# Pages in 32 partitions and dealt v rows in the sample's attention of a hybrid decoder step

## The reference

```
# the expert layer, for a block tb of 128 tokens, 128 chosen experts per token
act = gelu(einsum('thkd,td->thk', expert_u[eid], tb))
y   = einsum('thk,thkd->td', g * act, expert_v[eid])

# the sample's attention: 8 samples, each 32 pages of 128 tokens (256 + 32 words a token) and its new token
ckv_all = concatenate([cache_ckv[page_table].reshape(8, 4096, 256), ckv])
kr_all  = concatenate([cache_krope[page_table].reshape(8, 4096, 32), krope])
s = (q_abs . ckv_all + q_pe . kr_all) * scale        # the mask keeps every one of these tokens
o_lat = softmax(s) . ckv_all
```

## Time and profile before

| | us |
|---|---|
| median of 3 runs | 4161.53 |
| lowest, highest | 4159.66, 4172.78 |
| the profiled execution | 4134.78 |
| its span, first to last instruction | 4133.0 |
| granted clock of PE, mean | 0.918 |

### The profile page before, as it was taken

The page is one execution under the profiler, slowest core; times in us unless marked ns, Lnnn a source line. Parts: engine busy times, 40 slices in busy tenths (PEclk is TensorE's granted clock), DMA queues, the critical chain, the costliest instruction groups (busy, mean ns, idle before and its releaser), DMA issues.

```text
span 4133.0 us, 39221 instructions
## 1 busy us (share of the span) xinstructions
PE 3237.0 (78%) x11253; PEld 1588.6 (38%) x11253; DVE 2704.7 (65%) x6214; ACT 742.9 (18%) x2277; POOL 2527.7 (61%) x2069
## 2 busy tenths in 40 slices
PE   7887877876889876877988777877888777599954
PEld 3334333432344332433444233423344333366622
DVE  2156667767777568766886577756875577556554
ACT  2112111220112111211122022211122120111121
POOL 0005766777667767776667677666767677445462
PEclk9998999988999999889999999999999997799987
DMA  5668999999999999999999999999999999999996
GB/s 181 219 219 304 398 393 397 359 395 389 397 375 389 402 402 338 368 399 398 398 367 403 402 380 358 386 401 391 386 384 399 391 371 331 326 311 365 348 356 246
DMA packets 576043, 1489.93 MB, mean 360 GB/s; under 512 B 90267, under 2 KB 147236, under 8 KB 575812
## 3 DMA queue, kind: packets, MB, share of 16 engines
q0 software_dynamic: 297216, 1082.26, 68.3%
q1 hardware_dynamic: 238514, 392.77, 26.5%
q10 hardware_dynamic: 40098, 12.39, 1.3%
HBM read 1477.01 MB, written 10.20 MB: 360 GB/s over the span
## 4 chain that ended last, share of the span: by engine, by line
PE 36%; DMA 25%; POOL 17%; DVE 11%; issue 8%; ACT 3%; ACTq 1%; SPq 0%; POOLq 0%; DVEq 0%
DMA rows<-in_peer_v_dram,pe_id 16%; POOL rows L728 16%; PE PS L1190 12%; PE PS L823 11%; DMA rows<-in_peer_u_dram,pe_id 3%; PE PS L1107 3%; DVE rows L2148 3%; PE PS L832 2%; DMA wbuf<-in_w_out_dram 2%; PE PS L788 1%; DMA wbuf<-in_peer_w_q_dram 1%; DVE xr L2174 1%; PE PS L968 1%; PE PS L948 1%; DMA wbuf<-in_w_in_dram 1%
## 5 line engine op out<-in xcount | busy, mean ns | idle before, releaser
L728 POOL DMA_INDIRECT rows<-in_peer_u_dram,pe_id x1024 | 1259.9, 1230 | 880.0 <-DVE pe_id L1953 297.4
L1190 PE MATMUL PS<-rows,diags 128*128 128x512 f32 x2544 | 1344.0, 660 | 484.0 <-DMA rows<-in_peer_v_dram,pe_id 443.7
L728 POOL DMA_INDIRECT rows<-in_peer_v_dram,pe_id x1024 | 1248.3, 1219 | 671.6 <-DVE dots L2148 377.8
L2148 DVE CUSTOM_DVE_ANT_0 rows<-rows,px 128x1024 f32<-128x1024 f32 x1024 | 1242.0, 1223 | 525.0 <-DMA rows<-in_peer_u_dram,pe_id 520.4
L1190 PEld LDWEIGHTS PS<-rows,diags 128*128 128x128 f32 x2544 | 485.8, 206 | 1132.4 <-issue 979.2
L823 PE MATMUL PS<-wbuf,xt 128*128 128x512 f32 (+1 forms) x1696 | 780.4, 595 | 73.5 <-DMA wbuf<-in_w_in_dram 31.3
L2174 DVE SCALAR_TENSOR_TENSOR xr<-rows,gcoef,xr 128x1024 f32<-128x1024 f32 x388 | 498.3, 1284 | 149.1 <-issue 135.4
L823 PEld LDWEIGHTS PS<-wbuf,xt 128*128 128x128 f32 x1696 | 320.1, 196 | 494.3 <-issue 347.2
L823 PE MATMUL PS<-wbuf,wide 128*128 128x512 f32 (+1 forms) x736 | 341.6, 606 | 35.2 <-ACT wide L1301 14.8
L2254 ACT ACTIVATE diags<-ident,gcoef 128x128 f32<-128x128 f32 x636 | 231.4, 399 | 218.6 <-PE PS L1190 100.6
L823 PEld LDWEIGHTS PS<-wbuf,wide 128*128 128x128 f32 x736 | 143.6, 200 | 215.9 <-issue 162.5
(11 more groups left out here) (375 smaller groups left out, 2682.0 us busy)
## 6 DMA issues: line engine op xcount, KB each, us to landing
wbuf<-in_w_in_dram SPq DMA_DIRECT2D x274, 512.0 KB, 10.1
wbuf<-in_peer_w_q_dram SPq DMA_DIRECT2D x134, 512.0 KB, 12.1
wbuf<-in_w_ob_dram SPq DMA_DIRECT2D x66, 512.0 KB, 8.5
wbuf<-in_w_out_dram SPq DMA_DIRECT2D x66, 512.0 KB, 11.1
wbuf<-in_w_oa_dram SPq DMA_DIRECT2D x36, 512.0 KB, 8.1
rows<-in_peer_u_dram,pe_id POOLq DMA_INDIRECT x1028, 9.3
rows<-in_peer_v_dram,pe_id POOLq DMA_INDIRECT x1024, 9.3
KV<-in_cache_ckv_dram SPq DMA_DIRECT2D x128, 128.0 KB
```

Source lines behind the costliest of these rows:

```text
L728: pool.indirect_dma_start(row_slot(kind, n), None, a["peer_u" if kind == "u" else "peer_v"][0], bass.IndirectOffsetOnAxis(ap=pe_id[t % 2][ ...
L1190: last = nc.tensor.matmul(bank[3 + 4 * c], diag(n), row_slot("v", n)[:, c * 512:(c + 1) * 512], start=start, stop=stop)
L2148: V.tensor_tensor_reduce(out=row, in0=row, in1=px[:, :], scale=1.0, scalar=0.0, op0=ALU.mult, op1=ALU.add, accum_out=dots[:, at_:at_ + 1]) ...
```

## The change

Two things are edited. First, the copies of a page: before, page `k` of a group filled the columns `k` of all 128 partitions, one token to a partition, so a copy had 128 pieces of 1 KB (the rope part 128 of 128 B). Now page `k` fills the partitions 32k to 32k + 31 in full width, four tokens that follow each other in memory to a partition, so a copy has 32 pieces of 4 KB (the rope part 32 of 512 B). The place, size and semaphore of a group stay, and nothing that reads it is changed. Second, the table `LAST_ON_PE` is empty, as `LAST_ON_DVE` was.

```diff
@@ load_pages, SP
-                    sp.dma_start(page_at(g)[:, k * KVL:(k + 1) * KVL],
-                                 a["cache_ckv"][0][ds(page, 1)].rearrange("o p c -> (o p) c")).then_inc(s_pages[g % PAGE_SLOTS], 16)
+                    sp.dma_start(page_at(g)[32 * k:32 * (k + 1), :],
+                                 a["cache_ckv"][0][ds(page, 1)].rearrange("o (p s) c -> (o p) (s c)", s=4)).then_inc(s_pages[g % PAGE_SLOTS], 16)
...
-                        sp.dma_start(krope_at(g)[:, k * ROPE:(k + 1) * ROPE],
-                                     a["cache_krope"][0][ds(page, 1)].rearrange("o p c -> (o p) c")).then_inc(s_pages[g % PAGE_SLOTS], 16)
+                        sp.dma_start(krope_at(g)[32 * k:32 * (k + 1), :],
+                                     a["cache_krope"][0][ds(page, 1)].rearrange("o (p s) c -> (o p) (s c)", s=4)).then_inc(s_pages[g % PAGE_SLOTS], 16)
@@ load_ropes, ACT
-                    act.dma_start(krope_at(g)[:, k * ROPE:(k + 1) * ROPE],
-                                  a["cache_krope"][0][ds(page, 1)].rearrange("o p c -> (o p) c")).then_inc(s_pages[g % PAGE_SLOTS], 16)
+                    act.dma_start(krope_at(g)[32 * k:32 * (k + 1), :],
+                                  a["cache_krope"][0][ds(page, 1)].rearrange("o (p s) c -> (o p) (s c)", s=4)).then_inc(s_pages[g % PAGE_SLOTS], 16)
@@ tables
-LAST_ON_DVE, LAST_ON_PE = (74, 74), (17, 52)
+LAST_ON_DVE, LAST_ON_PE = (74, 74), (74, 74)
```

## The result

The changed kernel took 4209.09 us (median of 4 runs, 4201.58 to 4229.05) against 4161.38 us before (4 runs, 4159.66 to 4172.78): a ratio of 1.0120, 95% interval 1.0095 to 1.0144, some 48 us slower. The forecast was 4127.5 us with a range of 4106 to 4172, and its sign was wrong.

A forecast was written before the change was run, and what follows sets the result against it. PE was taken to bound the attention stage, with DMA close behind; limits of 272 and 267 us gave a 280 us stage, 32 us saved plus 2 for ACT: 4161.5 - 34 = 4127.5 us, range 4106 to 4172.

The forecast's parts named there:

- PE bounds the stage: Attention stage, 3603 to 3915 us: PE busy 297.7 of 312 us and alone in the chain of waits.
- The v rows take 63 us off PE: Attention stage: 35 v rows move to DVE; 312 - 63 = 249 us, with 3 us of waits per sample 272.
- rival E: Attention stage: a less busy PE is granted less clock, 0.90; stage 295 us, total 4144.5; chance 0.08.
- The floor of DMA, 287 us by 373 GB/s: Attention stage: 107.17 MB at the present packets' rate need 287 us, so the v rows alone gain 25.
- the page edit saves 19 us of DMA time: Attention stage: fewer, larger page and rope packets save 309 us over 16 engines, lowering DMA's limit from 287 to 268 us.
- Rival D: Attention stage: page copies at half rate, one after the other with the rest; stage 345 us, total 4194.5; chance 0.10.
- Its deciding point: Attention stage: D decides once pages and ropes land below 31.8 MB / (312 - 187) us = 254 GB/s.
- Rival C: Attention stage: page copies slowed, gathers filling the idle half; stage near 320 us, total 4169.5; chance 0.22.
- The retention part was set at nothing: Retention part, 3465 to 3577 us: shifted loads could move a meeting 10 us either way; counted as nothing.
- ACT's stall, 2 us: First sample's rope copies: fewer packets may free ACT's queue sooner, 0 to 6 us gained, 2 taken.
- The signs: Changed profile: L1190 down 140, L2174 at 423, last L1107 near 3880, 375 to 395 GB/s; wrong if 344, PE 80%.
- if q1 time per MB rises: Page queue in the stage: a rise, with PE waiting for DVE at L2087 and DVE for page copies, means C or D.

The follow-up runs named there:

- the second profile: The kernel before profiled once more with no edit: 4162.04 us, attention stage 319.8 us.
- experiment 2: Only the v rows' deal against the kernel before, pages and ropes as before: 4147.44 us, ratio 0.9960.
- experiment 8: Copies-only kernel, four page layouts alone, then beside row gathers: 397 GB/s for before's layout, 280 for 32 neighbouring partitions, 404 and 409 for every fourth and second.
- experiment 5: The changed kernel with a group's page and rope copies issued in the order 0, 2, 1, 3: 4200.21 us, ratio 1.0116 to the kernel before.
- experiment 9: Copies-only kernel beside gathers: 397 GB/s before's layout; 32 neighbouring partitions 282 (4 KB), 335 (1 KB), 300 (swapped order); 64 neighbouring 339.
- experiment 1: The page edit alone: the changed kernel with the old deal of v rows; 4209.44 us, ratio 1.0123 to the kernel before.
- experiment 3: The changed kernel with each page on every fourth partition and the old deal of v rows: 4178.46 us, ratio 1.0053 to the kernel before.
- experiment 4: The changed kernel with each page on every fourth partition, new deal of v rows kept: 4168.92 us, ratio 1.0016 to the kernel before.
- experiment 10: The kernel before with pages on 32 neighbouring partitions in 1 KB pieces, ropes likewise in 128 B, old deal: 4203.52 us, ratio 1.0129.

## Why the prediction was wrong, point by point

- **PE bounds the stage**: right for seven of the eight samples of before (300 of 320 us busy in the second profile too). "The chain of waits in this stage is PE alone" is a misreading: in the first sample it is ACT's queue (experiment 2). The base of 312 us was a favourable execution; the second profile, close to the median, has 320.
- **The v rows take 63 us off PE and come to 272 us with the hand-offs**: right in its mechanism, too large in size. Alone the stage came to 302, not 272, and the median to -13 us (ratio -17), where the text gave this edit 25. From the base of 320 the same sum gives 320 - 63 + 24 = 281. The other 21 us are PE's busy time above the sum; by the estimate above 13 of them are the clock, 0.93 instead of 0.98, which is rival E's mechanism. PE's idle time rose by 24 (20 to 44 us), just the 8 x 3 charged, but that is in part luck: little of it names DVE. DVE waited 49.5 us for L1107 there, not under 40.
- **The floor of DMA, 287 us by 373 GB/s**: not reached even alone; the best kernels ran 348 GB/s at 293 and 302 us. How much of that is DMA and how much the hand-offs isn't separated.
- **The step that failed: the page edit saves 19 us of DMA time.** It had the wrong sign. The packets fell as said (84510 to 40994), but a packet's time was priced as a matter of its size alone. The gain from size is nothing: beside gathers 1 KB pages on 128 partitions run at 397 GB/s, as much as gathers alone (396 and 389). The loss from the target is 397 to 280 GB/s.
- **Rival D** had it. Its sum, pages serial at half rate, said 345 us; the same sum with the bytes of after, (104.25 + 29.7) MB / 403, is 332; the 357 measured would take 375 GB/s in it, the kernel's mix being below what large packets reach. Its sign and mechanism stand, and its 4194.5 us is 15 below the median. Its deciding point, pages at less than 254 GB/s, was ill put: beside gathers before's pages come at 74 GB/s and near ones at 106 (experiment 8), and it is the total that falls. Its chance of 0.10 was too low, and the reason given for that, several page copies in flight on both sides, fell with experiments 5 and 9.
- **Rival C** assumed that gathers fill the idle half. They don't: the total falls, and the gathers' own packets go from 152 to 214 ns. The Trainium skill ("SBUF — State Buffer") has 32 neighbouring partitions reach 8 of 16 ports in the section "Door 1: The DMA port swizzle", and only 6% from two copies to different halves in the section "Can I just issue two DMAs to hit both halves?". The runs agree, with 282 against 397 GB/s and with 6% from the swapped order (300).
- **The retention part was set at nothing**: it lost 12 to 14 us. It took 141 us in the three kernels with near 4 KB pages (changed kernel, experiments 1 and 5) and 125 to 134 in all others, near in 1 KB pieces among them (134). That its eight groups of pages load beside the states is the likely reason; no run takes it apart.
- **ACT's stall, 2 us**: the stall did go. In the changed kernel the eight rope copies ahead of the queries take 5.11 us instead of 8.96 (8.20 in the second profile), and PE no longer waits for L1590; with DMA as the chain it gained nothing that can be seen. Where pages are as before, ACT's rope copies still hold 6.0% of the stage's chain in experiment 2 and 5.8% in the second profile of before.
- **The signs**: L1190 and L2174 came as said; the last L1107 started at 4004.4 instead of 3880; GB/s fell to 292 instead of rising, and PE was at 77%; the text's last sign of being wrong (344 GB/s, PE at 80%) was met and passed. PE's waits for DVE's maxima and weights, said to be 15 to 20 us, were 3 in after and 8 in experiment 2 (6.3 for L1129 and 1.2 for L1141). The text's own test, "if q1 time per MB rises", did not fire clearly: 31.1% x 357 / 29.24 MB = 3.8 us per MB against 30.5% x 312 / 31.25 = 3.0 in the earlier trace rows, a rise, but PE waited for v rows and not through L2087 for pages. The 4 KB pages took their time from the gathers.

What stays open: why copies to every fourth or second partition take longer to issue, and whether that alone makes the 18 us of experiment 3. Two things in the traces point there. SP's page copies take 472 ns in the median in the stages of experiments 3 and 4 and 333 ns in those of before and of experiment 2. And DVE waits longer ahead of its transposes for a releaser that the profile calls remote, another core or a queue that it doesn't know; experiment 2, then experiment 4:

```profile
DVE KV L2087 <- remote: 8.8, 4, 2.7
```

```profile
DVE KV L2087 <- remote: 27.2, 8, 6.5
```

In experiment 3 these are 29.4 us against 12.9 in the second profile of before, which has another 16.6 us ahead of L2087 with no cause named (3.7 in experiment 3). Later pages are likely, but no row names them.

## What to carry to other kernels

Before a copy is reshaped into larger packets, ask which partitions it lands on: pieces of 1 KB across all 128 partitions cost nothing beside large gathers here, while 4 KB pieces on 32 neighbouring ones took 30% of the total rate, and 1 KB pieces there cost the kernel as much. A copy alone, bound by its issue, doesn't show this; test it beside the traffic of its stage, and read GB/s, since the share stayed near 1 at 280 as at 400. Read the chain of a stage sample by sample: a bound that holds for seven of eight isn't the stage's. And of two edits made together measure each: here one was worth 0.4% and the other hid it; the deal with before's pages beats both kernels.

## What the runs showed of the hardware that was not expected

- A byte to 32 or 64 neighbouring partitions counts about twice: total rate x (1 + its share) = 394 to 413 GB/s in four mixtures; and the loss falls on all traffic in flight.
- Between experiments 1 and 10 packet size decided who waits: with 4 KB pages the gathers were late (28.1 us of PE's waits), with 1 KB pages the pages (2.7).
- Strided targets keep the total (404, 409 GB/s), but each copy takes 1.01 or 0.99 us instead of 0.86 alone, and the issue 472 ns instead of 333 in the kernel.
- Where PE had less to do in the stage its granted clock was lower in the mean over 2.4 and 1.2 GHz: 0.98 at 94% busy (before), 0.93 at 86% (experiment 2), 0.84 at 77% (changed kernel). The busy share alone doesn't fix it: experiment 5 had 0.89 at 77%, and the trunk 0.97 at 74%. The matmuls that stayed took part of the freed time back.
